# Mixture-of-experts block: which engine forms the low parts of the expert weights, in what pieces and in what order

## The reference, cut to what matters

```
for e in range(N_EXPERTS):                       # 16
    he = jax.nn.silu(h @ w1[e]) * (h @ w3[e])    # 1024 -> 512
    y = y + gates[:, e:e + 1] * (he @ w2[e])     # 512 -> 1024
```

## Time and profile before

| | us |
|---|---|
| median of 3 runs | 655.65 (653.96 to 656.15) |
| profiled execution, its own time | 651.59 |
| its span | 649.8 |
| TensorE busy | 543.9 (84%) |
| VectorE busy | 445.2 (69%) |
| ScalarE busy | 323.2 (50%) |
| GpSimd busy | 191.9 (30%) |
| sixteen DMA engines, HBM traffic over the span | 270 GB/s |

### The profile page before, as it was taken

How to read it: one execution, slowest core, us unless ns; L and a number is a source line. 1 busy time by engine, 2 the same in 40 slices (tenths; PEclk the granted TensorE clock), 3 DMA queues, 4 the chain that set the end, 5 groups by cost and what they waited for, 6 DMA issues and landing times.

```text
span 649.8 us, 7404 instructions
## 1 busy us (share of the span) xinstructions
PE 543.9 (84%) x2618; PEld 415.7 (64%) x2618; DVE 445.2 (69%) x577; ACT 323.2 (50%) x390; POOL 191.9 (30%) x141
## 2 busy tenths in 40 slices
PE   2789998984999899973899999999999999999820
PEld 2336845763776578851678778877877777877610
DVE  1366955427473634348788888899888899888527
ACT  4611223423426712234677678766667766767104
POOL 5003625221211400011234345543234443233040
PEclk9889999996999999965999999999999999999965
DMA  8999978390215601056789999999999999993156
GB/s 313 387 373 320 386 247 269 105 334 2 66 65 199 224 0 66 32 208 232 264 302 355 391 363 364 391 393 384 380 379 361 342 355 378 356 371 115 42 185 258
DMA packets 87832, 171.48 MB, mean 264 GB/s; under 512 B 5449, under 2 KB 17917, under 8 KB 87809
## 3 DMA queue, kind: packets, MB, share of 16 engines
q1 hardware_dynamic: 81410, 152.29, 66.1%
q10 hardware_dynamic: 2880, 10.49, 4.0%
q0 software_dynamic: 3520, 8.42, 3.6%
HBM read 158.58 MB, written 16.79 MB: 270 GB/s over the span
## 4 chain that ended last, share of the span: by engine, by line
PE 42%; DVE 25%; DMA 11%; issue 10%; SPq 6%; ACT 5%; POOL 0%; DVEq 0%; ACTq 0%; POOLq 0%
DMA ada<-in_ada_w 8%; DVE w_lo L1784 6%; DVE w_lo L1801 5%; DVE w_lo L1790 5%; PE psum L1118 3%; PE psum L1116 3%; PE psum L1117 3%; PE psum L1005 2%; SPq L520 2%; PE psum L1007 2%; PE psum L1006 2%; PE psum L882 2%; PE psum L1072 2%; PE psum L884 2%; PE psum L883 2%
## 5 line engine op out<-in xcount | busy, mean ns | idle before, releaser
L735 POOL TENSOR_TENSOR w_lo<-w,w_hi_a 128x1024 fp32r<-128x1024 f32 x15 | 46.5, 3098 | 162.0 <-ACT w_hi_a L1380 162.0
L1790 DVE TENSOR_TENSOR w_lo<-w,w_hi 128x1024 fp32r<-128x1024 f32 x64 | 76.4, 1237 | 0.0
L1801 DVE TENSOR_TENSOR w_lo<-w,w_hi 128x2048 fp32r<-128x2048 f32 x32 | 71.9, 2285 | 1.9 <-ACT w_hi L1393 1.9
L1384 ACT CAST w_hi<-w 128x2048 fp32r<-128x2048 f32 x32 | 61.0, 1908 | 17.6 <-PE psum L1101 16.7
L1784 DVE TENSOR_TENSOR w_lo<-w,w_hi_a 128x1024 fp32r<-128x1024 f32 x33 | 63.1, 1954 | 0.0
L1393 ACT CAST w_hi<-w 128x2048 fp32r<-128x2048 f32 x32 | 60.1, 1918 | 0.7 <-PE psum L1118 0.7
L1116 PE MATMUL psum<-w_hi,heT_hi 128*128 128x512 f32 x128 | 53.4, 417 | 2.9 <-DVE ysb L1822 1.8
L1118 PE MATMUL psum<-w_hi,heT_lo 128*128 128x512 f32 x128 | 50.8, 397 | 0.0
L1117 PE MATMUL psum<-w_lo,heT_hi 128*128 128x512 f32 x128 | 50.5, 395 | 0.0
L1089 PE MATMUL psum<-w_lo,xgT_hi 128*128 128x512 f32 x128 | 49.9, 390 | 0.0
L1099 PE MATMUL psum<-w_hi,xgT_hi 128*128 128x512 f32 x128 | 49.8, 389 | 0.0
(11 more groups left out here) (282 smaller groups left out, 1196.3 us busy)
## 6 DMA issues: line engine op xcount, KB each, us to landing
w<-in_moe_w SPq DMA_DIRECT2D x32, 2048.0 KB, 10.0
w<-in_moe_w SPq DMA_DIRECT2D x32, 1024.0 KB, 9.8
ada<-in_ada_w SPq DMA_DIRECT2D x12, 2048.0 KB, 18.1
win<-in_w_in SPq DMA_DIRECT2D x8, 1024.0 KB, 13.9
expert_rows<-ysb ACTq DMA_DIRECT2D x16, 512.0 KB, 7.6
expert_rows<-zero SPq DMA_DIRECT2D x1, 4096.0 KB, 17.8
wout<-in_w_out SPq DMA_DIRECT2D x4, 1024.0 KB, 5.0
x<-in_x SPq DMA_DIRECT2D x2, 1024.0 KB, 10.3
```

What stands on the lines that cost most here:

```text
L735: gp.tensor_tensor(w1_lo[b][:, k:k + 2, :], w1_sb[b][:, k:k + 2, :], w1_high(k, 2), ALU.subtract).then_inc(w1_lo_gp, 1)
L1384: act.copy(w3_hi[:, 4 * g:4 * g + 4, :].rearrange("p k f -> p (k f)"), w3_sb[b][:, 4 * g:4 * g + 4, :].rearrange("p k f -> p (k f)")).then ...
L1790: v.tensor_tensor(w3_lo[b][:, ks, :], w3_sb[b][:, ks, :], w3_hi[:, ks, :], ALU.subtract).then_inc(w3_lo_ok, 1)
L1801: v.tensor_tensor(w2_lo[b][:, :, hs], w2_sb[b][:, :, hs], w2_hi[:, :, hs], ALU.subtract).then_inc(w2_lo_ok[half], 1)
```

## The change

All of it is in the expert blocks.

- `low_w1` of GpSimd is gone. GpSimd copies the index column and gathers, no more.
- VectorE forms the low part of all of w1: groups 0 and 1 as one instruction of 128x2048, group 2, then `gated`, then group 3.
- VectorE forms `low_w3` groups 1 to 3 as one instruction of 128x3072.
- `expert_rows` of half 0 moves from behind `low_rows` to between the two `low_w2`.
- One semaphore counts all groups of w1; TensorE waits at k = 0 for two groups, at k = 4 and k = 6 for one each.

```diff
-            low_w1(1, 1)
             with gp.Fori(1, n_pairs) as i:
                 for b in range(2):
                     gather(b, i * 2 + b)
-                    low_w1(b, i * 2 + b)
...
                 for k in range(KD):
...
+                    if k in (0, 4, 6):
+                        pe.wait_ge(w1_lo_ok, s * 4 + (2 if k == 0 else 1 + k // 2))
...
+            def low_w1(b, s, g, n=1):
+                v.wait_ge(w1_hi_ok, s * 4 + g + n)
+                ks = slice(2 * g, 2 * (g + n))
+                v.tensor_tensor(w1_lo[b][:, ks, :], w1_sb[b][:, ks, :], w1_high(2 * g, 2 * n), ALU.subtract
+                                ).then_inc(w1_lo_ok, n)
+
+            def low_w3(b, s, g, n=1):
+                v.wait_ge(w3_hi_ok, s * 2 + 1 + (g + n - 1) // 2)
+                ks = slice(2 * g, 2 * (g + n))
                 v.tensor_tensor(w3_lo[b][:, ks, :], w3_sb[b][:, ks, :], w3_hi[:, ks, :], ALU.subtract
-                                ).then_inc(w3_lo_ok, 1)
+                                ).then_inc(w3_lo_ok, n)
...
             def block_(b, s, prev, prev_i, prev2):
                 if prev is not None:
-                    low_w1(b, s)
+                    low_w1(b, s, 0, 2)
+                    low_w1(b, s, 2)
                     gated(prev)
+                    low_w1(b, s, 3)
                     low_hidden(1 - b, prev)
                 if prev2 is not None:
                     expert_rows(b, prev2, None, 1)
                 if prev is not None:
                     low_w3(b, s, 0)
                 low_rows(s)
-                if prev is not None:
-                    expert_rows(1 - b, prev, prev_i, 0)
-                else:
-                    low_w1(b, s, range(3, 4))
+                if prev is None:
+                    low_w1(b, s, 3)
                     low_w3(b, s, 0)
-                for g in range(1, 4):
-                    low_w3(b, s, g)
+                low_w3(b, s, 1, 3)
                 if prev is not None:
                     low_w2(1 - b, prev, 1)
+                    expert_rows(1 - b, prev, prev_i, 0)
                 low_w2(b, s, 0)
...
-            low_w1(0, 0, range(3))
+            low_w1(0, 0, 0, 2)
+            low_w1(0, 0, 2)
```

More of the change, by code:

```diff
@@ L376, in build @@
         w1_hi_ok = sem("w1_hi_ok")
-        w1_lo_dve = sem("w1_lo_dve")
-        w1_lo_gp = sem("w1_lo_gp")
+        w1_lo_ok = sem("w1_lo_ok")
         w3_hi_ok = sem("w3_hi_ok")
```

## The result

| | before | changed |
|---|---|---|
| median, us | 655.59 (653.96 to 656.15, 4 runs) | 639.80 (635.94 to 640.67, 4 runs) |
| profiled execution, us | 651.59 | 639.7 |
| its span, us | 649.8 | 637.8 |
| ratio | | 0.9752, 95% interval 0.9708 to 0.9795 |

The change makes the kernel 2.5% faster, 15.8 us by the medians. (The kernel before has one run more here than in the table ahead of the prediction.)

The account below looks back on a forecast made before the run. TensorE was taken to wait for `he`, late because VectorE stands behind GpSimd's subtraction. 14 periods of 17.77 + 0.13 = 17.90 us against 19.10 save 16.8 us: 655.65 to 638.9, rounded to 639; forecast's range 637 to 642, outer 636 to 648.

Parts of the forecast that it names:

- TensorE's own 17.77 us: TensorE's work per regular expert block: a 19.44 us period less 1.67 us lost at the transposes of `he`.
- the 4.06 us: Median of the runs before above their profiled execution; unlocated in the profile, added to 634.8 us to give 638.9.
- The stall goes: VectorE's w1 pieces ahead of `he`: without GpSimd's subtractions, the 2.2 us stall behind GpSimd disappears.
- VectorE's work: VectorE's instructions per period sum to 16.84 us against 17.77, so it fits with 0.9 us for waits.
- The chain through the cast of w1: ScalarE's two casts, 2048 piece, group 2, then `he`: zero on paper, charged 0.0 to 0.3 us a period, 0.13 taken.
- Group 3 behind `gated`: VectorE's last w1 piece, 1.24 to 2.4 us after out1, is free inside a 1.37 us wait for ScalarE.
- the moved rows: `expert_rows` half 0 between the w2 pieces: done at 13.3 us, needed about 21.8, so hidden by 8 us.
- the merged pieces: w3 piece ends at 9.8 us, h3 wants it at 13.6; w1 piece: TensorE already waits for both groups. Free.
- the gather: GpSimd's copy and gather come some 18 us before the rows are needed, land in under 9, and cost nothing.
- the rival by which it would stall the path to h1: GpSimd's copy and gather hold VectorE 2.1 us near the first w3 piece and `low_rows`; 11 us slower, 667; chance 0.04.
- Block 0: No out1 hides `he` there, so it may be late once by 0 to 0.5 us; 0 taken.
- The loads: 7.1 MB a period at 391 GB/s just holds: cost 0, bounds 0 to 7 us; rival that they bind, chance 0.18.

Follow-up runs that it names:

- old order without GpSimd: Kernel before with all low parts on VectorE, in old pieces and old order, GpSimd only gathering; 659.92 us, ratio 1.0059 to the kernel before.
- GpSimd's groups kept: Changed kernel with w1 groups 2 and 3 back on GpSimd; 638.96 us, ratio 0.9750 to the kernel before.
- one merged piece: Kernel before with VectorE's two w1 pieces ahead of `he` as one 128x2048 instruction; 640.28 us, ratio 0.9776.
- one moved instruction: Kernel before with the half 0 output rows moved from behind the low rows to between the two w2 pieces; 639.73 us, ratio 0.9763.
- `he` first: Changed kernel with `he` ahead of w1 group 2 and group 3 behind the low rows; 639.12 us, ratio 0.9733 to the kernel before.
- small pieces: Changed kernel with w1 and w3 low parts in 128x1024 pieces again; 637.13 us, ratio 0.9700 to the kernel before.
- `he` first with the matmuls: Changed kernel with `he` ahead of w1 group 2, group 3 behind the low rows, and two more matmuls ahead of block 0's h1; 636.93 us, ratio 0.9708.

## Why the prediction was right, point by point

- **Time.** 639 forecast, 639.8 measured. Of the 16.8 us from the stage 15.95 came. The period was forecast at 17.90; it is 17.82 to 17.98 in most blocks, with three beyond: 18.43 behind block 1, whose transposes were 0.59 us late, 18.05 behind the next, and 18.26 where the load was late. TensorE's own 17.77 us hold (the shortest periods are 17.79 before and 17.82 here), though the sum behind them has a slip: the stretch to 491.16 ends 0.06 us behind out1, which starts at 491.10.
- **Luck in the time.** For the profiled execution the forecast was 634.8 us, and it measured 639.7: 0.9 us of the difference are in the stage, 3.0 ahead of it and 1.0 behind it. That the medians still agree within 1 us rests on the 4.06 us that the forecast carried over without a reason.
- **The stall goes.** Right as a row: L735 is gone, and so is the 2.2 us. But as a cause it was drawn too large. The sum took "GpSimd's subtractions go" as what frees `he`. The runs show that it is neither enough (old order without GpSimd: 659.9) nor needed (GpSimd's groups kept: 639.0; one merged piece: 640.3; one moved instruction: 639.7). What has to go is VectorE's standing behind GpSimd ahead of `he`.
- **VectorE's work** was 16.84 us in steps; the row shows 17.12 busy, because an instruction that has a wait behind it counts in full length. The 3072 piece steps 479.24 - 475.97 = 3.27, as taken, and is 3.35 us in full length.
- **The chain through the cast of w1.** `he` at +0.63 forecast, +0.69 measured in the block shown; lateness 0.13 a period forecast, 0.05 to 0.14 measured in 12 of 14 blocks, 0.59 and 0.33 in the others. One of the forecast's own signs of being wrong was `he` over 0.7 us behind out1: it is, mostly by under 0.1 us, in half the blocks, and by 1.22 and 0.96 us in two. The chain is real but worth little: with `he` first it is gone, and the time stays.
- **Group 3 behind `gated`, the moved rows, the merged pieces, the semaphore, the gather**: no wait for any of them. The gather came behind the transposes and held no instruction up; the rival by which it would stall the path to h1 didn't appear (`low_rows` takes 1.23 us).
- **Block 0.** 0 to 0.5 us forecast and taken as 0: TensorE waited for `he` 0.5 us longer there, and the low rows of block 1 came 3.02 us later than before, hardly more than the 2.95 by which h1 of block 0 ended late.
- **The loads** are the term whose size was off. The forecast had landing times grow by 0.25 us a period to 15.6, with no wait of ScalarE for a load, and named such a wait as a sign of being wrong. They grew by 0.6 from 13.1 and ended at 18.4, and ScalarE waited 1.3 and 0.2 us. The rate was right (389 to 392 from 362 to 523 us, then 381 to 385), but 7.1 MB in 17.88 us asks for 397 GB/s, and the landing times grew twice as fast as that difference gives; what makes up the rest is open. It cost 0.4 us here, and it bounds what lies beyond: small pieces, GpSimd's groups kept, `he` first, and `he` first with the matmuls have `he` in time, let ScalarE wait 4.1 to 4.2 us for w, and all end at a mean period of 17.98 to 18.00 us.
- **The 4 us between the profiled execution and the median before**, carried over unexplained, are probably in part the granted clock in block 0: it costs h1 1.6 us in the profile of the changed kernel (7.2 in place of 5.6), and of 11 profiles only that of the kernel before was spared. This is argued, not shown, as no slower execution of the kernel before has a profile; the rest is not located.

## What to carry to other kernels

When two engines exclude each other, ask which of them may stand, before asking which should do the work: a gap between two instructions of the critical one lets in another that is already waiting, and one longer instruction, or a start half a microsecond earlier, can be worth as much as moving all of the other's work. A wait of half a microsecond for something unrelated, early in a queue, can lose such a race later in it. And when a version gets faster, compute at once what the loads need per period: here it was 2% above what they sustain, so that what `he` first saved early was given back at the end.

## What was not expected of the hardware

- Which of the two stands turned on half a microsecond. With GpSimd arriving 0.5 us behind the start of VectorE's pair, VectorE stood in 11 blocks of 12 (4.56 us in place of 2.35); with 0.9 us or more, in 1 of 18.
- GpSimd's copy of one index column takes 0.18 us, and mostly 0.85 to 1.19 where VectorE is subtracting beside it.
- Matmuls that compute nothing, 1.9 us of them in a wait of 2.4 us, kept the granted clock at 1.00 and gained some 3 us.
